# Sparse-attention heads of a fused four-layer kernel: order of the scores, row sums, gates and the position column

## The reference

```
proj = h @ w_in                                     # queries, 6 groups of keys/values, gates
k_c = gelu((blocks(k) + pe_k) @ w1_k) @ w2_k        # compression: 15 blocks of 32 tokens
v_c = gelu((blocks(v) + pe_v) @ w1_v) @ w2_v
for each of 16 heads (4 heads share a key group):
  s_c = q k_c - slope * distance, s_s = q k_s - slope * distance, s_w = q k_w - slope * distance
  p   = exp(s - max) / sum(exp(s - max))            # masked, for each of the three
  o   = gate0 * (p_c v_c) + gate1 * (p_s v_s) + gate2 * (p_w v_w)
x = x + o @ w_out
```

## Time and profile before

| | |
|---|---|
| median of 3 runs | 2898.27 us (2896.77 to 2900.39) |
| the profiled execution | 2905.14 us, its span 2903.3 us |
| busy: PE, PEld, DVE, ACT | 2622.9 us (90%), 2208.2 (76%), 1318.2 (45%), 410.4 (14%) |
| mean granted TensorE clock | 0.922 of 2.4 GHz |
| NSA layer, first load to the end of the loop | 2252 to 2617 us of the span |

### The profile page before, as it was taken

One profiled execution on the slowest core, in us unless ns is written; L12 is line 12 of the kernel. 1 busy time (PEld: TensorE's weight loads), 2 busy tenths in 40 slices (PEclk: granted clock), 3 DMA queues, 4 the chain that ended last, 5 costly groups with the idle time before them and its releaser, 6 DMA issues.

```text
span 2903.3 us, 36963 instructions
## 1 busy us (share of the span) xinstructions
PE 2622.9 (90%) x15394; PEld 2208.2 (76%) x15394; DVE 1318.2 (45%) x2563; ACT 410.4 (14%) x1246; POOL 206.4 (7%) x208
## 2 busy tenths in 40 slices
PE   7989999999995998999999999757998697778998
PEld 5558999999985756999999999544665577665665
DVE  4735848788541651957878843142000002321001
ACT  2121111101000220211111110120000002220000
POOL 0000022122110000012222210000000000000000
PEclk9999999999997999999999999888999795558999
DMA  5314689999994221669999998311442430001442
GB/s 188 116 58 160 242 339 402 394 389 418 421 419 167 100 104 58 217 261 376 391 379 412 420 421 342 141 62 71 146 159 87 157 117 1 1 0 76 155 153 93
DMA packets 84670, 625.20 MB, mean 215 GB/s; under 512 B 10353, under 2 KB 13016, under 8 KB 14116
## 3 DMA queue, kind: packets, MB, share of 16 engines
q1 hardware_dynamic: 53060, 418.21, 37.4%
q0 software_dynamic: 28032, 201.54, 17.1%
q10 hardware_dynamic: 3424, 3.27, 0.3%
HBM read 621.72 MB, written 1.06 MB: 215 GB/s over the span
## 4 chain that ended last, share of the span: by engine, by line
PE 83%; DMA 7%; DVE 6%; ACT 2%; issue 1%; SPq 0%; ACTq 0%; DVEq 0%; PEldq 0%
PE bank L651 19%; PE bank L675 15%; PE bank L402 9%; PE bank L416 8%; PE bank L424 8%; PE bank L390 7%; DMA weight_ring<-in_experts 5%; PE bank L665 5%; PE bank L354 3%; PE bank L818 2%; PE bank L772 2%; PE bank L845 1%; PE bank L847 1%; PE bank L471 1%; DMA sub_keys_T<-in_subk_h 1%
## 5 line engine op out<-in xcount | busy, mean ns | idle before, releaser
L675 PE MATMUL bank<-arena,weight_ring 128*128 128x160 f32 x4096 | 575.4, 300 | 13.6 <-DMA weight_ring<-in_experts 13.4
L675 PEld LDWEIGHTS bank<-arena,weight_ring 128*128 128x128 f32 x4096 | 558.7, 190 | 22.5 <-DMA weight_ring<-in_experts 22.5
L651 PE MATMUL bank<-hidden_T,weight_ring 128*128 128x160 f32 x4096 | 569.8, 301 | 1.0 <-ACT arena L1013 0.9
L651 PEld LDWEIGHTS bank<-hidden_T,weight_ring 128*128 128x128 f32 x4096 | 560.7, 191 | 2.2 <-issue 2.0
L1571 DVE CUSTOM_DVE_ANT_0 arena<-arena 128x1024 f32<-128x1024 f32 x192 | 234.5, 1221 | 202.7 <-DMA arena<-in_expert_rows,choice_by_pair 202.7
L390 PE MATMUL bank<-weight_ring,hidden_T 128*128 128x512 f32 (+1 forms) x544 | 234.6, 588 | 36.4 <-DVE hidden_T L1695 34.3
L402 PE MATMUL bank<-hidden_T,weight_ring 128*128 128x256 f32 (+1 forms) x1088 | 251.9, 394 | 4.7 <-DVE hidden_T L1186 4.7
L885 POOL DMA_INDIRECT arena<-in_expert_rows,choice_by_pair x192 | 199.3, 1038 | 776.4 <-DVE arena L1584 701.7
L354 PE MATMUL bank<-identity,arena 128*128 128x128 f32 (+4 forms) x428 | 89.6, 379 | 176.4 <-DVE arena L1173 111.2
L402 PEld LDWEIGHTS bank<-hidden_T,weight_ring 128*128 128x128 f32 (+1 forms) x1088 | 210.1, 195 | 41.9 <-DVE hidden_T L1186 7.1
L1584 DVE SCALAR_TENSOR_TENSOR arena<-arena,pair_weights 128x1024 f32<-128x1024 f32 x188 | 240.6, 1280 | 0.2
(11 more groups left out here) (310 smaller groups left out, 1914.5 us busy)
## 6 DMA issues: line engine op xcount, KB each, us to landing
weight_ring<-in_experts SPq DMA_DIRECT2D x256, 1024.0 KB, 9.1
weight_ring<-in_mlp SPq DMA_DIRECT2D x64, 1024.0 KB, 4.8
weight_ring<-in_dense_h SPq DMA_DIRECT2D x22, 2048.0 KB, 7.7
weight_ring<-in_dense_nsa SPq DMA_DIRECT2D x9, 2048.0 KB, 7.8
weight_ring<-in_dense_rg SPq DMA_DIRECT2D x7, 2048.0 KB, 7.7
arena<-in_expert_rows,choice_by_pair POOLq DMA_INDIRECT x192, 11.0
arena<-distance_bias_scratch ACTq DMA_DIRECT2D x2, 768.0 KB, 19.7
residual<-in_x SPq DMA_DIRECT2D x1, 1024.0 KB
```

What stands on the lines that cost most here:

```text
L651: last = mm(bank[s % 2][:, 0:DT_TOK], w[:, k * P:(k + 1) * P], HT[:, k, 0:DT_TOK], start=k == 0, stop=k == KD - 1)
L675: last = mm(bank[4 + k // 2][:, (k % 2) * DT_TOK:(k % 2 + 1) * DT_TOK], w[:, k * P:(k + 1) * P], HACT[:, s, :], start=s == 0 and k % 2 == ...
```

## The change

It does five things, all in the NSA layer:
1. PE issues the scores of heads 0 and 1 first, and then for each h: turn(h), values(h-1), scores(h+2). DVE's list becomes bend(0), bend(1), then combine(h-1), bend(h+2). `SB` becomes three heads deep.
2. The compressed keys are placed in front of and behind the window keys (`KW`), so the scores are four products (128, 256, 143 and 271 columns) where there were six; `dcon` has 798 columns for this, instead of 414.
3. The values get a 65th column of ones, so that each product also gives the row sum; the exponentials no longer sum.
4. The probabilities are not scaled. Each branch and tile has its own place in bank 6 or 7, and `nsa_combine` multiplies the six products by gate over sum (into `CM`) and adds the three branches. turn(h) waits for the exponentials only.
5. The position term is loaded into a third part of `ZC` and is a third group of 15 columns of the compression's products, the separate products of one column go; three memsets are added at the start of DVE's list.

```diff
-        ZC = at6(4, T)
-        KS = at6(2, NG, T)
-        VS = at6(2, TT, 256)
+        ZC = at6(2, 3, T)
+        KS = at6(NG, T)
+        KW = at6(NG, NC + T + NC)
+        VS = at6(2, TT, NG, HD + 1)
-        SB = at6(2, 800)
+        SB = at6(3, 798)
+        CM = at6(2, 6, HD)
-        dcon = at6(414)
+        dcon = at6(798)
...
-                        mm(bank[2 * w + half][0:64, 0:30].rearrange("p (c n) -> p c n", n=NC), w1[p0:p0 + 64, w, r, :],
-                           ZC[p0:p0 + 64, 2 * w:2 * w + 2, r:r + 16 * (NC - 1) + 1:16], start=r == 0, stop=r == 31)
-                for r in range(32):
-                    for half in range(2):
-                        p0 = 64 * half
-                        last = mm(bank[2 * w + half][0:64, 32:33], w1[p0:p0 + 64, w, r, :], pe_T[p0:p0 + 64, w, r:r + 1],
-                                  start=r == 0, stop=r == 31)
+                        last = mm(bank[2 * w + half][0:64, 0:45].rearrange("p (c n) -> p c n", n=NC), w1[p0:p0 + 64, w, r, :],
+                                  ZC[p0:p0 + 64, w, :, r:r + 16 * (NC - 1) + 1:16], start=r == 0, stop=r == 31)
...
+                q = [Q8[p0:p0 + 64, h // 2, tt * P:(tt + 1) * P] for tt in range(TT)]
+                o = bank[2 * h % 4]
+                mm(o[:, 0:P], q[0], KS[p0:p0 + 64, g, 0:P], start=True, stop=True)
+                mm(o[:, P:384], q[1], KS[p0:p0 + 64, g, 0:T], start=True, stop=True).then_inc(S["nsa_scores"], 1)
+                o = bank[2 * h % 4 + 1]
+                mm(o[:, 0:NC + P], q[0], KW[p0:p0 + 64, g, 0:NC + P], start=True, stop=True)
+                mm(o[:, NC + P:414], q[1], KW[p0:p0 + 64, g, NC:NC + T + NC], start=True, stop=True).then_inc(S["nsa_scores"], 1)
...
-                pe.wait_ge(S["nsa_scaled"], h + 1)
+                pe.wait_ge(S["nsa_probs"], h + 1)
...
-                if h % 4 == 0 and g >= 2:
-                    pe.wait_ge(S["nsa_copied"], g - 1)
+                if h >= 2:
+                    pe.wait_ge(S["nsa_copied"], h - 1)
+                o = bank[6 + h % 2][:, 0:390].rearrange("p (n d) -> p n d", n=6)
                 for tt in range(TT):
-                    o = bank[6 + g % 2][:, tt * 256 + (h % 4) * HD:tt * 256 + (h % 4 + 1) * HD]
                     for br in range(2):
                         for j in range(tt + 1):
-                            mm(o, PTN[:, h % 2, br * 512 + (tt + j) * P:br * 512 + (tt + j + 1) * P],
-                               VS[:, br, j, g * HD:(g + 1) * HD], start=br + j == 0, stop=False)
-                    last = mm(o, PTN[0:NC, h % 2, tt * 512 + 384:tt * 512 + 512], VC[0:NC, x, :], start=False, stop=True)
+                            mm(o[:, 2 * br + tt, :], PTN[:, h % 2, br * 512 + (tt + j) * P:br * 512 + (tt + j + 1) * P],
+                               VS[:, br, j, g, :], start=j == 0, stop=j == tt)
+                    last = mm(o[:, 4 + tt, :], PTN[0:NC, h % 2, tt * 512 + 384:tt * 512 + 512], VC[0:NC, x, :], start=True, stop=True)
...
             nsa_scores(0)
+            nsa_scores(1)
             for h in range(NH):
-                if h + 1 < NH:
-                    nsa_scores(h + 1)
                 nsa_turn(h)
                 if h:
                     nsa_values(h - 1)
+                if h + 2 < NH:
+                    nsa_scores(h + 2)
             nsa_values(NH - 1)
-            pe.wait_ge(S["nsa_copied"], NG)
+            pe.wait_ge(S["mix_part"], 1)
...
-                    last = A(s[:, c0:c1], s[:, c0:c1], ACT.Exp, bias=m[:, n:n + 1], accum_out=stat[:, 64 + 8 * (h % 2) + n:65 + 8 * (h % 2) + n])
+                    last = A(s[:, c0:c1], s[:, c0:c1], ACT.Exp, bias=m[:, n:n + 1])
...
+            add(V.memset(ZC[:, :, 2, 32:T], 0.0))
+            add(V.memset(VS[:, :, :, :, HD:HD + 1].rearrange("p b t g d -> p (b t g) d"), 1.0))
+            add(V.memset(VC[0:NC, :, HD:HD + 1], 1.0))
...
-            add(V.tensor_copy(KC, bank[4][:, 0:60]))
+            by_group = bank[4][:, 0:60].rearrange("p (a b n) -> p b a n", a=2, b=2)
+            for c0 in (0, NC + T):
+                add(V.tensor_copy(KW[:, :, c0:c0 + NC].rearrange("p (b a) n -> p b a n", a=2), by_group))
...
-            def nsa_scale(h):
...
+            def nsa_combine(h):
+
+                dve.wait_ge(S["nsa_product"], h + 1)
+                o = bank[6 + h % 2][:, 0:390].rearrange("p (n d) -> p n d", n=6)
+                r, cm = stat[:, 96 + 8 * (h % 2):102 + 8 * (h % 2)], CM[:, h % 2, :, :]
+                link(V.reciprocal(r.unsqueeze(2), o[:, :, HD:HD + 1]))
                 link(V.tensor_tensor(r, r, GV[:, h, :], ALU.mult))
+                V.tensor_tensor(cm, o[:, :, 0:HD], bc(r.unsqueeze(2), [P, 6, HD]), ALU.mult).then_inc(S["nsa_copied"], 1)
+                dve.wait_ge(S["nsa_copied"], h + 1)
+                last = V.tensor_reduce(OA[:, :, h * HD:(h + 1) * HD], cm.rearrange("p (b t) d -> p t d b", t=2), AX.X, ALU.add)
...
+            nsa_bend(0)
+            nsa_bend(1)
             for h in range(NH):
-                nsa_bend(h)
                 if h:
-                    nsa_scale(h - 1)
-                if h >= 6 and h % 4 == 2:
-                    nsa_copy((h - 6) // 4)
-            nsa_scale(NH - 1)
-            nsa_copy(NG - 1)
+                    nsa_combine(h - 1)
+                if h + 2 < NH:
+                    nsa_bend(h + 2)
+            nsa_combine(NH - 1)
```

More of the change, by code:

```diff
@@ L205, in program @@
         CBIAS = at6(4)
-        KC = at6(60)
-        VC = at6(4, HD)
+        VC = at6(4, HD + 1)
         ncol = at6(16)
@@ L809, in nsa_scores @@
                 g, p0 = h // 4, 64 * (h % 2)
-                x = (g % 2) * 2 + g // 2
                 if h >= 2:
                     pe.wait_ge(S["nsa_biased"], 2 * h - 2)
[L814 to L821, removed]
+                q = [Q8[p0:p0 + 64, h // 2, tt * P:(tt + 1) * P] for tt in range(TT)]
[5 more added lines that the diff above has]
+                mm(o[:, NC + P:414], q[1], KW[p0:p0 + 64, g, NC:NC + T + NC], start=True, stop=True).then_inc(S["nsa_scores"], 1)
             def nsa_turn(h):
-                pe.wait_ge(S["nsa_scaled"], h + 1)
+                pe.wait_ge(S["nsa_probs"], h + 1)
                 if h:
                     pe.wait_ge(S["nsa_PT"], h)
-                s = SB[:, h % 2, :]
+                s = SB[:, h % 3, :].rearrange("p (b n) -> p b n", b=2)
                 for br in range(2):
                     for j in range(3):
-                        turn(bank[4 + br][:, j * P:(j + 1) * P], s[:, br * 384 + j * P:br * 384 + (j + 1) * P])
-                    last = turn(bank[4 + br][0:NC, 384:512], s[:, 768 + NC * br:768 + NC * (br + 1)])
+                        turn(bank[4 + br][:, j * P:(j + 1) * P], s[:, br, j * P:(j + 1) * P])
+                    last = turn(bank[4 + br][0:NC, 384:512], s[:, br, 384:399])
                 last.then_inc(S["nsa_turned"], 1)
@@ L1100, in _ @@
             stages.n = 0
-            for dst, name in ((ncol, "cols_nsa"), (nrow, "rows_nsa"), (pe_T, "pe_nsa"), (W2[0:64], "w2_nsa"), (dcon, "c_distance"),
+            for dst, name in ((ncol, "cols_nsa"), (nrow, "rows_nsa"), (ZC[:, :, 2, 0:32], "pe_nsa"), (W2[0:64], "w2_nsa"), (dcon, "c_distance"),
                               (valid, "c_valid")):
@@ L1107, in _ @@
                 out_half(b, Q8[:, 4 * b:4 * b + 2, :].rearrange("p a b -> p (a b)"), scale=HD ** -0.5)
-            out_half(2, ZC[:, 0:2, :].rearrange("p a b -> p (a b)"))
+            out_half(2, ZC[:, 0, 0:2, :].rearrange("p a b -> p (a b)"))
             for b in (3, 4):
                 act.wait_ge(S["proj_done"], 2 * b + 1)
-                A(VS[:, b - 3, :, :].rearrange("p a b -> p (a b)"), bank[b - 3][:], ACT.Copy)
-                out_half(b, KS[:, b - 3, 0:2, :].rearrange("p a b -> p (a b)"))
+                A(VS[:, b - 3, :, :, 0:HD].rearrange("p t g d -> p (t g) d"), bank[b - 3][:].rearrange("p (n d) -> p n d", d=HD), ACT.Copy)
+                A((KS[:, 0:2, :] if b == 3 else KW[:, 0:2, NC:NC + T]), bank[4 + 2 * (b % 2)][:].rearrange("p (g t) -> p g t", g=2),
+                  ACT.Copy).then_inc(S["proj_out_act"], 1)
             act.wait_ge(S["nsa_gates"], 2)
@@ L1722, in _ @@
             for x in range(4):
[L1723 removed]
+                add(V.tensor_copy(CBIAS[0:64, x:x + 1], bank[x][0:64, 30:31]))
             sync()
@@ L1836, in constants @@
     i = np.arange(P)[:, None]
-    d = np.concatenate([i - np.arange(P), P + i - np.arange(T), i - (np.arange(NC) * 16 + 31), P + i - (np.arange(NC) * 16 + 31)], 1)
+    key, late, end = i - np.arange(P), P + i - np.arange(T), np.arange(NC) * 16 + 31
+    d = np.concatenate([key, late, i - end, key, late, P + i - end], 1)
     c["c_distance"] = np.where(d >= 0, d, -NEG).astype(np.float32)
```

44 lines of the change are left out of this document (17 added, 27 removed).

## The result

| | before | after |
|---|---|---|
| median, runs alternating on one chip | 2899.33 us (2896.77 to 2905.18, 4 runs) | 2831.69 us (2823.06 to 2836.25, 4 runs) |
| ratio, 95% interval | | 0.9758 [0.974, 0.9777] |
| profiled execution, its span | 2905.14, 2903.3 us | 2823.06, 2821.3 us |
| mean granted clock | 0.922 | 0.936 |

The profiled execution of after is the shortest of its four, that of before lies 6 us over its median. Pieces are compared between traces, whole times between medians.

What follows compares the result with a forecast made beforehand. One wait per head for DVE and PE's own work at 1.2 GHz bound the loop. Terms -59.5 - 13.4 + 0.2 + 0.7 + 0.5 + 0.9 = -70.6 took the 2898.3 us median to 2828, range 2798 to 2848.

Steps and rivals of the forecast that it cites:

- The loop: NSA head loop, first score to transposes: 142.6 us instead of 202.1, -59.5, with PE's cycle at 8.75 us.
- the 65th column: Values products in the loop: the added column costs nothing, upper bound 16 instructions a head x 0.002 us.
- What the prediction said of change 1: Loop: turn(h) needs only exponentials whose scores were issued two heads before, so PE's 3.5 us wait a head goes.
- Compression: NSA compression: one-column products removed, 45 columns stay under the weight load as halves overlap; -13.4 us, +6 without overlap.
- 0.50 from compression to the transposes: Sign to check in the changed kernel: granted clock 0.50 from the compression, through the loop, to the transposes.
- The start: Start of the NSA layer: larger loads +0.7 us (0 to 2), three memsets ahead of the norm +0.5 us.
- The clock behind the loop: Output projection behind the loop: the clock's rise may fall elsewhere against the shifted work, 0 to +2.6 us, taken +0.9.
- The sum: Whole kernel: all terms together -70.6 us, the median going from 2898.3 to 2828 us.
- B: Loop: two heads of lead do not cover ACT's and DVE's chain; 2842 us at 1 us wait, 2856 at 2; 12%.
- C: Loop products: reads of 65-wide rows and keys beginning 15 columns in are slow; 2908 us at 0.25 us each; 2%.
- D: Loop: turn(h) still waits as long each head, only compression and fewer score products count; 2876 us; 3%.
- A: Clock rises in the loop: 2780 us if all at 2.4 GHz, 2795 to 2818 if partly; 16%, 5 for all.

Runs made afterwards that it cites:

- e3: The kernel before, with DVE scaling each head ahead of the next head's bend and `SB` three deep; 2850.83 us, ratio 0.9821.
- e12: The kernel after, with the scores of head h+1 issued between turn(h) and values(h-1); 2855.76 us, ratio 0.9847.
- e5: The kernel after, with score products over all 128 partitions, the keys stored twice with zeros in opposite halves; 2777.64 us, ratio 0.9563.
- e4: The kernel after, with the compression's 32 products of one partition half ahead of the 32 of the other, not alternating; 2838.73 us, ratio 0.9782.
- e1: The kernel before, with change 5 alone (position term as a third group of columns in the compression); 2887.89 us, ratio 0.9957.
- e7: The kernel after, with the layer's norm waiting only for its own 8 KB load and the other five awaited behind it; 2815.43 us, ratio 0.9698.
- e2: The kernel after, with its loops written one head ahead; the engines' lists came out identical, so it repeats after; 2829.57 us, ratio 0.9757.
- e8: The kernel after, unchanged, measured again in the second group; 2824.93 us, ratio 0.9734.
- e6: The kernel after, with the compression reading 15 neighbouring columns instead of every 16th, giving another result; 2824.44 us, ratio 0.9728.

## Why the prediction was right, point by point

**The loop** (changes 1 to 4, forecast 142.6 us and -59.5): 142.8 and -59.35. PE's cycle was put at 8.75 and is 8.73; the first score to turn(0) at 6.8 and is 6.96 (2399.99 - 2393.03); exponentials at 1.8, they take 1.90; PE without a wait for ACT or DVE, as it came. The bounds for what no row of before showed have closed on the chosen values: `nsa_combine` 1.6 us (0.20 and 0.17 for the small ones, 0.558 and 0.595 for the two of 384 elements):

```profile
L1769 DVE TENSOR_REDUCE arena<-arena 128x128 f32<-128x384 f32 x13 | 7.7, 595 | 0.5
L1767 DVE TENSOR_TENSOR arena<-bank,statistics 128x384 f32<-128x384 f32 x13 | 7.3, 558 | 0.4
```

and the 65th column nothing:

```profile
L838 PE MATMUL bank<-arena 128*128 128x65 f32 x156 | 38.0, 414 | 0.0
```

(groups of the loop: count, busy us, mean ns, idle before). The values with 64 columns took 417 ns in before.

**What the prediction said of change 1** is wrong in its reason, though the size came out. It has turn(h) need only exponentials "whose scores were issued two heads before", as if the new order gave that; the order of TensorE's list is that of before, letter for letter. The size is right because the step that was costed, a wait of 3.5 us for bend(h+1) and scale(h), does go, by change 4 alone as far as the loop's lists tell: after and before differ in DVE's list by combine in the scaling's place. Writing both lists out for three heads would have shown it. e3 shows the place of the scaling to be the cause of the wait, e12 what the order of the scores is worth.

**Compression** (forecast -13.4, with +6 if the halves did not overlap): -16.7 in the profile, and this is the term that was mis-sized. The overlap is right: e5, whose clock fell 0.7 us into the compression, has it in 13.5 us at 1.2 GHz, 53 ns an instruction, as forecast; e4, with the halves apart, needs 25.9. What the forecast took over from before without asking is the clock of 0.50. In the compression of after it is 1.00, and there an instruction takes 39.5 ns, so 10.3 us. So the sign "0.50 from compression to the transposes" did not come. Eleven profiled executions here have 45 columns and alternating halves. All enter the compression at 1.00; in ten the clock falls only 11.1 to 12.2 us after the first product, when the last is through, in e5 after 0.7 us. In before, e3 (both with 30 columns and 1) and e4 it falls after 0.5 to 0.9 us. Whether the 45 columns are the cause, these runs don't show. Against the medians e1 puts the whole edit at -13.7, with an interval of -17.4 to -7.5, in which both -13.4 and -16.7 lie.

**The start** (+1.2 forecast, from +0.7 for the loads and +0.5 for memsets): +0.9. The larger load landed later as forecast, by 0.24 us (17.45 against 17.21) and not 0.7:

```profile
arena<-in_c_distance ACTq DMA_DIRECT2D x1, 399.0 KB, 17.6
```

and the memset of 448 columns takes 0.43 us. e7 shows what that sum walked past: the norm needs none of the loads that it was costing, and waiting for its own alone is worth 9.5 us between the medians.

**The clock behind the loop** (+0.9, between 0 and 2.6): the output projection takes 29.76 us instead of 27.75, +2.0, since the clock rose at 2544.4, 4 us into it; inside the range, and smaller than what the profiled execution won elsewhere behind the loop (-1.1 in all). The 16 transposes, behind which the prediction saw the clock rise, end here at 2539.5 with 0.50.

**The sum** of the forecast was -70.6. The medians differ by 67.6, 72.1 (e2) and 77.1 (e8) in three measurements of the same program, 2831.69, 2829.57 and 2824.93 us; the profile's two terms, -59.35 and -16.7 with +0.9 and +2.0, make -73. So more agreement than some 5 us can't be claimed. That 2828 lies 4 us from the first median is in part luck: the loop agrees by itself, but the 3 us that the compression's clock gave and the forecast didn't have lie within what one measurement of the same program differs from another.

**The rivals.** *B*, the cover is too short: no wait of a turn in the loop, as the 5.8 us of chain against 8.75 of cover said; e12, with 3.9 of cover, has that wait. *C*, slow reads: rows of 65 cost nothing (414 against 417 ns), and the four products of a head, two of them on keys that begin 15 columns in, take the 2.95 us that were costed at 2.9; a stride does cost, 10 ns an instruction in the compression, but the loop has none. *D*: excluded by 8.73. *A*, the clock rises in the loop: it did not, at 113.00 of 113.00 us busy. The reason given for that in the prediction (the scores fill half of the partitions) was only argued there; e5 changes nothing else in TensorE's list, and the clock rises. There A's price holds too: 5.15 us a head and 2777.6 us, against 5.3 and 2780. The Trainium skill, "TensorE: Matmul & The Clock Gate", § What's actually happening, has activity release the clock; taken as busy time alone it doesn't fit these rows: busy all the time at 0.50 in after, busy 92% at 1.00 in e5.

**What stays open.** Why e5's compression lost the clock when ten others kept it, though its code there is that of after, and whether the 45 columns are what kept it in the ten. What each of changes 2, 3 and 4 brings alone. Whether filled partitions of the scores are what counts, or their stationary part of 128 by 128, which e5 brings with them. Why e4's 15.7 us of longer compression show as 7 to 14 in the medians. Why e6 pauses. The projections' earlier rise of the clock in after (-1.7) was not tried. Whether `SB` has to be three deep was not tried; by the lists, turn(h) is through before scores(h+2) start, so two should do. A version with the scores' halves of two heads issued alternately, which would need no second copy of the keys, was not run.

## What to carry to other kernels

Write each engine's list out for three heads before and after: a loop that is said to issue work further ahead may be the old list cut elsewhere, and a wait of 3.5 us a head may be one pair of steps in the wrong order on VectorE. A stretch of TensorE work that is always busy can still sit at half clock; where products fill 64 of 128 partitions, filling the others with zeros costs TensorE no instruction (VectorE and ScalarE some memsets and copies ahead of the loop) and was worth 47 us here, after which the order of the other engines' lists has to be read again (8.5 us more). And wait for each load where it is used: one wait for six loads cost some 10 us (9.5 between the medians, 13.5 in the traces) in front of a norm that needs 8 KB.

## What the runs showed of the hardware that was not expected

- With the scores over 64 partitions the granted clock was 0.50 with TensorE busy 113.00 of 113.00 us (after); with the same scores over 128 it was 1.00 with 64.28 of 70.00 (e5), and 0.50 again from 2481.1, when the last scores (start 2476.2) were through and TensorE had begun to wait.
- Moving data with a stride of 16 columns of float32 took 39.5 ns an instruction of 45 columns, neighbouring columns 29.2 ns, both at 2.4 GHz with alternating halves. At 1.2 GHz 30 and 45 strided columns and a single one all took 53 ns; 45 neighbouring columns were not run at that clock.
- Products of 64 x 64 that alternate between the halves of the partitions overlap: 53 ns alternating and about 102 ns apart, both at 1.2 GHz.
- With 45 columns and alternating halves the clock stayed 1.00 through the compression in ten of eleven profiled executions; with 30 and 1 (before, e3), and with the halves apart (e4), it fell to 0.50 within its first us. The cause is open.
